# A side program of sliding-window attention in 18 steps in place of 26, at a lower rate of steps

## The chip, the cores and the metric

The kernel runs on one core of a Trainium2 chip. The metric is the device time of one execution in microseconds. The kernel before takes 1376.13 us, the median of three runs (1376.1 to 1376.48).

## The reference

One pass over 512 positions of width 1024 through a block with three mixers, a feed-forward layer with a short convolution, then an mLSTM layer and a layer of dilated attention. The change touches the part of the first block that computes two of the mixers. The sliding-window attention has 8 query heads of width 64 over 2 key heads, in query blocks of 128 positions that each read their own key block and the one before:

```python
s = jnp.einsum('bnqhgd,bnkhd->bnhgqk', qb, kw)
s = jnp.where(valid[None, :, None, None], s, -jnp.inf)
m = jnp.maximum(jnp.max(s, axis=-1, keepdims=True), sink)
p = jnp.exp(s - m)
denom = jnp.sum(p, axis=-1, keepdims=True) + jnp.exp(sink - m)
o = jnp.einsum('bnhgqk,bnkhd->bnqhgd', p / denom, vw)
```

The gated linear attention (GLA) beside it works in chunks of 64 positions with a decay per channel; its output is normalised per head and multiplied by `silu(r)`. The output of each mixer goes through a projection and is multiplied by a sigmoid gate, and the three are added.

## The kernel before

The stream of the large products is what the whole kernel is built around. All weights stand as 128x128 blocks in one long row (`wall`), eight to a unit of 512 KB. SP loads a unit into one of three buffers `raw`; ACT rounds it to fp32r (`WH`, a CAST at L189), DVE computes the rest (`WL = raw - WH`, L152); PE then multiplies each block three times, `HH,WH`, `HL,WH` and `HH,WL` (the activations are split in the same way), each 128x512 (`passes`, L205 is the line of the helper that issues all of them). One block is three matmuls. A tile of the output is 8 blocks of an input of width 1024 or 4 of one of width 512, and takes one of three PSUM banks in turn.

Everything that is no large product is written as a Python generator, a side program, once for each engine: PE, DVE, ACT and POOL each have their own `swa_side()` and `gla_side()`, whose steps (the code between two `yield`) have to be cut alike. The place of a step in the stream is the same on all engines. `tile` calls `pump(0.25)` after every second block; `pump` adds `rate * share` to a counter and takes one step from the first side program of the list for each whole that it holds. With a rate of 1.7 that is 0.425 of a step per turn of two blocks. `tokens` (the four tiles of GLA's values, 32 blocks of weights) makes sixteen such turns, and the narrow tile `glow` four. `later()` runs other short pieces once or twice a tile.

So a step on DVE or ACT stands in its instruction order between the work for the tiles around it: rounding the weights (`CAST WH`, `WL`), and taking finished tiles out of PSUM. Each engine works its list in order, and waits for the others by semaphores.

The sliding attention has eight pieces (`i` from 0 to 7: four query blocks `n`, two pairs of heads `jp`). The parts of one piece, with the engine:

- `scores(i)`: PE, 8 matmuls `ps<-SKT,SQT` (4 for each `ps` bank) into banks 3 and 4 of PSUM. DVE then adds the mask into `SC` (L152), takes the maximum (L170) and three small ones; ACT takes four exponentials of `SC` with their sums (`exps(i)`, L202); DVE divides `SC` by the sum (three instructions, the last `SC<-SC,sm`).
- the transposes of the piece: PE, 8 `ps<-ident,SC` (L209) into banks 5 and 6, and ACT copies them into `PTT` (L189).
- `values(i)`: PE, 16 matmuls `ps<-PTT,SVT` into bank 7; ACT rounds the result into `PH`, DVE computes `PL`.

In each round PE issues `scores(i + 1)`, then in the next step `values(i - 1)`, and in a third one the transposes of `i`. With one step ahead of the rounds and one behind them that makes 26 steps.

GLA follows in the same list. It has two pairs of heads `pr`; for each there are seven levels of masked products in `level(pr, lv)` (PE `ps<-GQK` and `ps<-gqks`, two levels in every second step; POOL and DVE prepare a decay `gE`, ACT takes its exponential, DVE multiplies `gqks<-GQK,gE` and picks the result into `gA`), then the states (`gS`), the outputs (`go`, in banks 3 and 4), and the normalisation: squares, transposes and a sum (`sm`, L170), ACT `Sqrt`, DVE reciprocal (L183), two transposes `ps<-ident,sm` on PE that spread the factor as a row, an ACT copy `RT<-ps`, and DVE `gon<-ps,cv,RT` (L164), which frees the bank of `go`. The first step of levels of the pair `pr = 1` writes into those banks.

The stream beside them: the tile `glow` (blocks 80 to 88), four tiles `gq`, `gk` (to 120), the value tiles (to 152), `branch(0)` (to 248: tiles of 8 and 4 blocks in turn), four tiles `r` (to 280), `branch(1)` (to 376), where POOL also adds into `X` after every second tile.

Of the kernel before, what the change touches and what calls it, by code (L numbers as in the profile page):

```python
# [603 lines left out]
def build(nc, a_in):  # L604
    with ExitStack() as ctx:
# [275 lines left out]
        def pe_program(p):  # L881
# [18 lines left out]
            def swa_side():  # L900
                def scores(i):
                    n, jp = divmod(i, 2)
                    W = 128 if n == 0 else 256
                    k0 = 0 if n == 0 else (n - 1) * P
                    two = [p.fill(SB[g], ("ss", i, g)) for g in range(2)]
                    for jj in range(2):
                        j = 2 * jp + jj
                        p.wait_ge(S.dve, "sq", j)
                        for g in range(2):
                            p.matmul(two[g][:, jj * 256:jj * 256 + W], SQT[64 * g:64 * g + 64, j, n * P:(n + 1) * P],  # L910
                                     SKT[64 * g:64 * g + 64, k0:k0 + W], True, True)
                            if jj:
                                p.then_inc(("ss", i, g))

                def values(i):
                    n, jp = divmod(i, 2)
                    W = 128 if n == 0 else 256
                    k0 = 0 if n == 0 else (n - 1) * P
                    s = p.fill(SB[4], ("so", i))
                    p.wait_ge(S.act, "ptt", i, 1)  # L920
                    for jj in range(2):
                        for q in range(W // P):
                            kb = k0 // P + q
                            p.wait_ge(S.act, "sv")
                            for g in range(2):
                                p.matmul(s[64 * g:64 * g + 64, jj * P:(jj + 1) * P], SVT[:, kb, 64 * g:64 * g + 64],
                                         PTT[:, 2 * g + jj, q * P:(q + 1) * P], q == 0, q == W // P - 1).then_inc(("so", i))

                scores(0)
                yield  # L930
                for i in range(8):
                    n, jp = divmod(i, 2)
                    W = 128 if n == 0 else 256
                    sc = SCS[i % 2][:, :, 0:W]
                    if i < 7:
                        scores(i + 1)
                    yield
                    if i > 0:
                        values(i - 1)
                    yield  # L940
                    for g in range(2):
                        s = p.fill(SB[2 + g], ("st", i, g))
                        p.wait_ge(S.dve, "sn", i)
                        for jj in range(2):
                            for q in range(W // P):
                                p.transpose(s[:, jj * 256 + q * P:jj * 256 + (q + 1) * P], sc[:, 2 * g + jj, q * P:(q + 1) * P], ident)
                        p.then_inc(("st", i, g))
                    yield
                values(7)
                yield  # L950
                p.mark("swa")

            def decays():
                for pr in range(2):
# [217 lines left out]
            p.soon.append(sv_turn())  # L1172
            for j in range(4):
                p.tile(("sq", j), H_mix)
            p.rate = 1.7
            swa = swa_side()
            p.side.append(swa)
            p.narrow(("glow",), H_mix)
# [281 lines left out]
        def dve_program(v):  # L1460
# [17 lines left out]
            def swa_side():  # L1478
                def scores(i):
                    n, jp = divmod(i, 2)  # L1480
                    W = 128 if n == 0 else 256
                    sc = SCS[i % 2][:, :, 0:W]
                    mx, nm, sume, den, es = swa_cols(i)
                    for g in range(2):
                        x = ps("ss", i, g).rearrange("p (j k) -> p j k", j=2)[:, :, 0:W]
                        m = swm[:, 256 - W:256].rearrange("p (o k) -> p o k", o=1).to_broadcast([P, 2, W])
                        v.wait_ge(S.pe, "ss", i, g)
                        v.wait_ge(S.consts, "consts")
                        if i > 1:
                            v.wait_ge(S.pe, "st", i - 2, 1)  # L1490
                        v.tensor_tensor(sc[:, 2 * g:2 * g + 2, :], x, m, ADD).then_inc(("sc", i, g), free("ss", i, g))
                    sinks = cv[:, COL["sinks"] + 4 * jp:COL["sinks"] + 4 * jp + 4]
                    v.wait_ge(S.dve, "sc", i, 1)
                    v.tensor_reduce(mx, sc, MAX).then_inc(("smx", i))
                    v.wait_ge(S.dve, "smx", i)
                    v.tensor_tensor(mx, mx, sinks, MAX).then_inc(("smx2", i))
                    v.wait_ge(S.dve, "smx2", i)
                    v.tensor_scalar(nm, mx, -1.0, MUL).then_inc(("snm", i))
                    v.wait_ge(S.dve, "snm", i)
                    v.tensor_tensor(es, sinks, nm, ADD).then_inc(("ses", i))  # L1500

                def values(i):
                    n, jp = divmod(i, 2)
                    hi = PH[:, 4 + 2 * jp:6 + 2 * jp, n * P:(n + 1) * P]
                    lo = PL[:, 4 + 2 * jp:6 + 2 * jp, n * P:(n + 1) * P]
                    v.wait_ge(S.act, "so hi", i)
                    v.tensor_tensor(lo, ps("so", i)[:, 0:256].rearrange("p (j k) -> p j k", j=2), hi.bitcast(F32),
                                    SUB).then_inc(("sy", i), free("so", i))

                scores(0)  # L1510
                yield
                for i in range(8):
                    W = 128 if i < 2 else 256
                    sc = SCS[i % 2][:, :, 0:W]
                    mx, nm, sume, den, es = swa_cols(i)
                    v.wait_ge(S.act, "sexp", i)
                    v.tensor_tensor(den, sume, es, ADD).then_inc(("sden", i))
                    v.wait_ge(S.dve, "sden", i)
                    v.reciprocal(den, den).then_inc(("srcp", i))
                    v.wait_ge(S.dve, "srcp", i)  # L1520
                    v.tensor_tensor(sc, sc, den.rearrange("p (h o) -> p h o", o=1).to_broadcast([P, 4, W]), MUL).then_inc(("sn", i))
                    if i < 7:
                        scores(i + 1)
                    yield
                    if i > 0:
                        values(i - 1)
                    yield
                    yield
                values(7)
                yield  # L1530
                v.mark("swa")

            def gla_side():
                def output(h):
# [378 lines left out]
            for j in range(4):  # L1913
                v.tile(8)
                v.wait_ge(S.pe, "sq", j)
                v.scalar_tensor_tensor(SQT[:, j, :], ps("sq", j), 0.125, RS, MUL, MUL).then_inc(("sq", j), free("sq", j))
            v.rate = 1.7
            swa = swa_side()
            v.side.append(swa)
            v.tile(8)  # L1920
# [335 lines left out]
        def act_program(a):  # L2256
# [8 lines left out]
            def swa_side():  # L2265
# [10 lines left out]
                def values(i):  # L2276
                    n, jp = divmod(i, 2)
                    a.wait_ge(S.pe, "so", i)
                    a.copy(PH[:, 4 + 2 * jp:6 + 2 * jp, n * P:(n + 1) * P],
                           ps("so", i)[:, 0:256].rearrange("p (j k) -> p j k", j=2)).then_inc(("so hi", i))  # L2280
# [2 lines left out]
                yield  # L2283
                for i in range(8):
                    W = 128 if i < 2 else 256
                    yield
                    if i > 0:
                        values(i - 1)
                    if i < 7:
                        exps(i + 1)  # L2290
                    yield
                    for g in range(2):
                        a.wait_ge(S.pe, "st", i, g)
                        if i > 0:
                            a.wait_ge(S.pe, "so", i - 1)
                        x = ps("st", i, g).rearrange("p (j k) -> p j k", j=2)[:, :, 0:W]
                        a.copy(PTT[:, 2 * g:2 * g + 2, 0:W], x).then_inc(("ptt", i, g), free("st", i, g))
                    yield
                values(7)
                yield  # L2300
                a.mark("swa")

            def decays():
                yield
# [248 lines left out]
            a.soon.append(sv_turn())  # L2553
            for _ in range(4):
                a.tile(8)
            a.rate = 1.7
            swa = swa_side()
            a.side.append(swa)
            a.tile(8)
# [247 lines left out]
        def pool_program(g):  # L2807
# [21 lines left out]
            def swa_side():  # L2829
                yield  # L2830
                for i in range(8):
                    yield
                    yield
                    yield
                yield
                g.mark("swa")

            def gla_side():
                def open_level(pr, lv):
# [54 lines left out]
            g.side.append(pool)  # L2894
            for _ in range(5):
                g.tile(8)
            g.rate = 1.7
            swa = swa_side()
            g.side.append(swa)
            g.tile(8)  # L2900
# [403 lines left out]
```

## Time and profile before

| | us |
|---|---|
| median of three runs | 1376.13 |
| the profiled execution | 1375.52 |
| its span, first to last instruction | 1373.7 |
| PE busy (matmuls) | 1363.2 (99%) |
| PEld busy (weight loads) | 1112.9 (81%) |
| DVE busy | 842.8 (61%) |
| ACT busy | 603.5 (44%) |
| POOL busy | 180.4 (13%) |

The profiled execution is one run of the same program, taken by the hardware profiler; its time of 1375.52 us is 0.61 us below the median. Busy time is the time in which an engine has an instruction in flight. Matmuls overlap: one 128x512 matmul is shown with some 0.39 us and the next starts 0.23 us later, so a busy PE can still lose time between two starts, and starts are the better measure of it. The chain that ended last has 87% of the span on PE, 8% on DVE, 2% on ACT.

### The profile page before, as it was taken

The numbers are of one execution on the slowest core, as the hardware profiler recorded it, in microseconds if no ns is written. First come the engines' busy times: TensorE is split into PE (matmuls) and PEld (weight loads), VectorE is DVE, ScalarE is ACT, GpSimd is POOL, SyncE is SP. The second block draws the span as 40 slices with busy tenths as digits, with TensorE's granted clock in tenths as the row PEclk, the third lists the DMA queues.
The fourth block names the chain that finished last, engine by engine and source line by source line (L and its number), as shares of the span: only waits on it lengthen the run. The fifth ranks groups of instructions, "written<-read, shape, count | busy, mean of one in ns | idle before, by whom it ended". The sixth has DMA issues, their size and how long they took to land.

```text
span 1373.7 us, 17229 instructions
## 1 busy us (share of the span) xinstructions
PE 1363.2 (99%) x6752; PEld 1112.9 (81%) x6752; DVE 842.8 (61%) x1233; ACT 603.5 (44%) x922; POOL 180.4 (13%) x149
## 2 busy tenths in 40 slices
PE   9999999999999999999999999999999999999998
PEld 8777788788888788888888888888888888787887
DVE  6565575854343697624776456746455676877775
ACT  5355433333245454423444345434554544344551
POOL 0300010212311300000000112000001120243330
PEclk9999999999999999999999999999999999999999
DMA  6322222223352433332333324522225233212132
GB/s 213 123 78 77 78 78 62 78 76 94 93 184 77 138 108 108 108 103 82 92 106 94 110 80 150 154 77 77 62 65 175 82 122 100 89 62 63 47 138 77
DMA packets 37817, 136.55 MB, mean 99 GB/s; under 512 B 4452, under 2 KB 5476, under 8 KB 37096
## 3 DMA queue, kind: packets, MB, share of 16 engines
q1 hardware_dynamic: 37440, 134.39, 30.8%
q8 instruction: 53, 0.87, 0.3%
q10 hardware_dynamic: 296, 1.06, 0.2%
q14 instruction: 28, 0.23, 0.1%
HBM read 129.14 MB, written 6.30 MB: 99 GB/s over the span
## 4 chain that ended last, share of the span: by engine, by line
PE 87%; DVE 8%; ACT 2%; issue 2%; DMA 1%; POOL 0%; DVEq 0%; SPq 0%; ACTq 0%; POOLq 0%
PE ps L205 84%; PE ps L209 2%; DVE WL L152 2%; DVE TT L164 2%; DVE HL L164 1%; DMA kept<-PW 1%; DVE X L152 1%; DVE KT L164 0%; ACT WH L189 0%; ACT L202 0%; DVE sm L170 0%; DMA raw<-in_wall 0%; ACT HH L202 0%; DVE gqks L152 0%; ACT row L202 0%
## 5 line engine op out<-in xcount | busy, mean ns | idle before, releaser
L205 PE MATMUL ps<-HH,WH 128*128 128x512 f32 (+1 forms) x1096 | 437.4, 401 | 0.7 <-DVE HL L164 0.6
L205 PE MATMUL ps<-HL,WH 128*128 128x512 f32 (+1 forms) x1096 | 423.4, 388 | 0.0
L205 PE MATMUL ps<-HH,WL 128*128 128x512 f32 (+1 forms) x1080 | 417.6, 388 | 0.0
L152 DVE TENSOR_TENSOR WL<-raw,WH 128x1024 fp32r<-128x1024 f32 (+1 forms) x221 | 282.0, 1281 | 78.2 <-ACT WH L189 77.1
L189 ACT CAST WH<-raw 128x1024 fp32r<-128x1024 f32 (+1 forms) x222 | 231.1, 1042 | 133.9 <-PE ps L205 114.7
L205 PEld LDWEIGHTS ps<-HH,WH 128*128 128x128 f32 x1096 | 205.9, 188 | 48.2 <-issue 6.4
L205 PEld LDWEIGHTS ps<-HL,WH 128*128 128x128 f32 x1096 | 206.2, 188 | 41.4 <-issue 1.9
L205 PEld LDWEIGHTS ps<-HH,WL 128*128 128x128 f32 x1080 | 202.7, 188 | 42.9
L205 PE MATMUL ps<-PH,WH 128*128 128x512 f32 x424 | 167.0, 394 | 0.0
L205 PE MATMUL ps<-PH,WL 128*128 128x512 f32 x424 | 165.2, 390 | 0.0
L205 PE MATMUL ps<-PL,WH 128*128 128x512 f32 x424 | 165.1, 389 | 0.0
L152 POOL TENSOR_TENSOR SQS<-SQS,SQ 128x512 f32<-128x512 f32 x47 | 72.0, 1532 | 677.3 <-ACT SQ L202 676.7
L152 DVE TENSOR_TENSOR TH<-ps,RS 128x512 f32<-128x512 f32 (+1 forms) x93 | 63.6, 684 | 132.7 <-PE ps L205 124.0
L205 PEld LDWEIGHTS ps<-PH,WL 128*128 128x128 f32 x424 | 79.6, 188 | 16.8
L205 PEld LDWEIGHTS ps<-PH,WH 128*128 128x128 f32 x424 | 79.6, 188 | 16.6 <-issue 0.7
L205 PE MATMUL ps<-WH,HH 128*128 128x512 f32 x224 | 91.9, 410 | 0.6 <-DVE WL L152 0.3
L205 PEld LDWEIGHTS ps<-PL,WH 128*128 128x128 f32 x424 | 79.7, 188 | 15.8
L205 PE MATMUL ps<-WL,HH 128*128 128x512 f32 x224 | 87.4, 390 | 0.0
L205 PE MATMUL ps<-WH,HL 128*128 128x512 f32 x224 | 87.3, 390 | 0.0
L202 ACT ACTIVATE TH<-TH 128x512 f32<-128x512 f32 (+1 forms) x41 | 25.5, 621 | 102.1 <-DVE TH L152 102.1
L164 DVE SCALAR_TENSOR_TENSOR CT<-TH,cv,CT 128x511 f32<-128x511 f32 x88 | 65.8, 748 | 6.5 <-ACT CT L202 5.0
L202 ACT ACTIVATE CT<-TH,cv 128x512 f32<-128x512 f32 x44 | 36.0, 818 | 56.7 <-DVE TH L152 54.6
(224 smaller groups left out, 1440.6 us busy)
## 6 DMA issues: line engine op xcount, KB each, us to landing
raw<-in_wall SPq DMA_DIRECT2D x221, 512.0 KB, 3.6
kept<-PW SPq DMA_DIRECT2D x2, 2048.0 KB, 8.9
PWR<-kept SPq DMA_DIRECT2D x2, 2048.0 KB, 7.9
X<-in_xT SPq DMA_DIRECT2D x8, 256.0 KB, 4.1
X<-in_xT SPq DMA_DIRECT2D x4, 512.0 KB, 5.7
out_T<-X SPq DMA_DIRECT2D x7, 256.0 KB, 2.0
pe<-in_pT SPq DMA_DIRECT2D x2, 512.0 KB, 4.9
MB<-mrow ACTq DMA_DIRECT2D x1, 1024.0 KB, 4.8
```

Source lines behind the costliest of these rows:

```text
L152: return self.put(None if self.e is None else self.e.tensor_tensor(out, x, y, op))
L164: return self.put(self.e.scalar_tensor_tensor(out=out, in0=x, scalar=s, in1=y, op0=op0, op1=op1))
L189: return self.put(None if self.e is None else self.e.copy(out, x))
L202: return self.put(self.e.activation(out, x, f, **kw))
L205: return self.put(None if self.e is None else self.e.matmul(out, l, r, start=start, stop=stop, skip_group_check=True))
L209: return self.put(None if self.e is None else self.e.transpose(out, x, ident[0:k, 0:k]))
```

## The change

On every engine the step with `values(i - 1)` and the one with `scores(i + 1)` become one, values first. A round has two steps in place of three, the whole 18 in place of 26. The rate of steps is 1.15 from the start of the sliding attention, and 1.7 again when its last step has returned, which is seen only when the next step is asked for.

```diff
--- before.py
+++ after.py
@@ -932,11 +932,10 @@
                     n, jp = divmod(i, 2)
                     W = 128 if n == 0 else 256
                     sc = SCS[i % 2][:, :, 0:W]
+                    if i > 0:
+                        values(i - 1)
                     if i < 7:
                         scores(i + 1)
-                    yield
-                    if i > 0:
-                        values(i - 1)
                     yield
                     for g in range(2):
                         s = p.fill(SB[2 + g], ("st", i, g))
@@ -949,6 +948,7 @@
                 values(7)
                 yield
                 p.mark("swa")
+                p.rate = 1.7
 
             def decays():
                 for pr in range(2):
@@ -1172,7 +1172,7 @@
             p.soon.append(sv_turn())
             for j in range(4):
                 p.tile(("sq", j), H_mix)
-            p.rate = 1.7
+            p.rate = 1.15
             swa = swa_side()
             p.side.append(swa)
             p.narrow(("glow",), H_mix)
@@ -1525,10 +1525,10 @@
                     if i > 0:
                         values(i - 1)
                     yield
-                    yield
                 values(7)
                 yield
                 v.mark("swa")
+                v.rate = 1.7
 
             def gla_side():
                 def output(h):
@@ -1914,7 +1914,7 @@
                 v.tile(8)
                 v.wait_ge(S.pe, "sq", j)
                 v.scalar_tensor_tensor(SQT[:, j, :], ps("sq", j), 0.125, RS, MUL, MUL).then_inc(("sq", j), free("sq", j))
-            v.rate = 1.7
+            v.rate = 1.15
             swa = swa_side()
             v.side.append(swa)
             v.tile(8)
@@ -2283,12 +2283,11 @@
                 yield
                 for i in range(8):
                     W = 128 if i < 2 else 256
-                    yield
                     if i > 0:
                         values(i - 1)
+                    yield
                     if i < 7:
                         exps(i + 1)
-                    yield
                     for g in range(2):
                         a.wait_ge(S.pe, "st", i, g)
                         if i > 0:
@@ -2299,6 +2298,7 @@
                 values(7)
                 yield
                 a.mark("swa")
+                a.rate = 1.7
 
             def decays():
                 yield
@@ -2553,7 +2553,7 @@
             a.soon.append(sv_turn())
             for _ in range(4):
                 a.tile(8)
-            a.rate = 1.7
+            a.rate = 1.15
             swa = swa_side()
             a.side.append(swa)
             a.tile(8)
@@ -2831,9 +2831,9 @@
                 for i in range(8):
                     yield
                     yield
-                    yield
                 yield
                 g.mark("swa")
+                g.rate = 1.7
 
             def gla_side():
                 def open_level(pr, lv):
@@ -2894,7 +2894,7 @@
             g.side.append(pool)
             for _ in range(5):
                 g.tile(8)
-            g.rate = 1.7
+            g.rate = 1.15
             swa = swa_side()
             g.side.append(swa)
             g.tile(8)
```

No instruction is added or removed; their order changes. Three places show it.

PE, in `branch(0)`, at the values of piece 5 (`ps<-PTT,SVT`). Before:

```order
L205 MATMUL ps<-HL,WH 128x512
L205 MATMUL ps<-HH,WL 128x512
L205 MATMUL ps<-PTT,SVT 64x128 x8
L205 MATMUL ps<-HH,WH 128x512
L205 MATMUL ps<-HL,WH 128x512
```

Now:

```order
L205 MATMUL ps<-HL,WH 128x512
L205 MATMUL ps<-HH,WL 128x512
L205 MATMUL ps<-PTT,SVT 64x128 x8
L205 MATMUL ps<-SKT,SQT 128x256 x4
L205 MATMUL ps<-HH,WH 128x512
L205 MATMUL ps<-HL,WH 128x512
```

The scores of piece 7 (`ps<-SKT,SQT`) stood alone twelve matmuls ahead of the values; now they follow them without a matmul of the stream between. The same holds for six rounds, `i` from 1 to 6.

ACT, at the end of the first GLA pair (`RT<-ps` copies the rows, `PH<-RG` rounds the output, `TH` is the tanh of a tile, the table load goes with `Sqrt` and with the tanh after it). Before:

```order
L202 ACT_TABLE_LOAD
L202 ACTIVATE sm<-sm,cv 128x8
L189 COPY RT<-ps 128x512
L189 CAST PH<-RG 128x512
L202 ACT_TABLE_LOAD
L202 ACTIVATE TH<-RG 128x512
L189 CAST WH<-raw 128x1024
L189 COPY RT<-ps 128x512
L189 CAST PH<-RG 128x512
```

Now:

```order
L202 ACT_TABLE_LOAD
L202 ACTIVATE sm<-sm,cv 128x8
L202 ACT_TABLE_LOAD
L202 ACTIVATE TH<-RG 128x512
L189 CAST WH<-raw 128x1024
L189 COPY RT<-ps 128x512
L189 CAST PH<-RG 128x512
L189 COPY RT<-ps 128x512
L189 CAST PH<-RG 128x512
```

The tanh of the last `r` tile and a rounding of weights stood between the two row copies; now both stand ahead of the first, and the two copies have only `PH<-RG` between them.

POOL, at the second GLA pair (`gb_93` is its decay). Before:

```order
L152 TENSOR_TENSOR gE_83<-gb_93 128x8x32
L152 TENSOR_TENSOR gE_84<-gb_93 128x16x16
L152 TENSOR_TENSOR gE_83<-gb_93 128x32x8
L152 TENSOR_TENSOR gE_84<-gb_93 128x64x4
L152 TENSOR_TENSOR X<-X,TT 128x512
L152 TENSOR_TENSOR gE_83<-gb_93 128x128x2
L152 TENSOR_TENSOR gE_84<-gb_93 128x256
L152 TENSOR_TENSOR X<-X,TT 128x512 x15
```

Now:

```order
L152 TENSOR_TENSOR gE_83<-gb_93 128x8x32
L152 TENSOR_TENSOR gE_84<-gb_93 128x16x16
L152 TENSOR_TENSOR gE_83<-gb_93 128x32x8
L152 TENSOR_TENSOR X<-X,TT 128x512
L152 TENSOR_TENSOR gE_84<-gb_93 128x64x4
L152 TENSOR_TENSOR gE_83<-gb_93 128x128x2
L152 TENSOR_TENSOR gE_84<-gb_93 128x256
L152 TENSOR_TENSOR X<-X,TT 128x512 x15
```

The first addition into `X` stood behind the fourth preparation `gE`, and now stands ahead of it, behind the third.

## Rows read from the trace of the kernel before

**Rows 1.** The page's first part: the span, and busy time of each engine.

```profile
span 1373.7 us, 17229 instructions
PE 1363.2 (99%) x6752; PEld 1112.9 (81%) x6752; DVE 842.8 (61%) x1233; ACT 603.5 (44%) x922; POOL 180.4 (13%) x149
```

**Rows 2.** Two stretches, columns: us; PE, PEld, DVE, ACT, POOL busy (x instructions); clock; DMA.

```profile
66.00:178.00 112.00, 112.00 (x613) 86.69 (x612) 66.51 (x114) 56.46 (x131) 0.00 (x0) 1.00 0.26 81
238.00:300.00 62.00, 59.84 (x499) 48.24 (x499) 43.24 (x71) 23.96 (x34) 12.67 (x8) 1.00 0.22 69
```

**Rows 3.** Who waited for whom, PE: us in total, times, longest.

```profile
PE ps L205 <- DVE gon L164: 1.5, 1, 1.5
```

**Rows 4.** PE in order of time, 149 to 152 us: start, us, engine, instruction.

```profile
149.84 0.39 PE L205 MATMUL ps<-PL,WH 128*128 128x512 f32 x1
150.07 0.39 PE L205 MATMUL ps<-PH,WL 128*128 128x512 f32 x1
150.39 1.14 PE L205 MATMUL ps<-SKT,SQT 64*128 64x256 f32 x8
151.45 0.50 PE L205 MATMUL ps<-HH,WH 128*128 128x512 f32 x1
151.79 0.40 PE L205 MATMUL ps<-HL,WH 128*128 128x512 f32 x1
```

**Rows 5.** PE in order of time: four transposes alone, and four beside two others.

```profile
1166.62 0.60 PE L209 MATMUL ps<-ident,SQ 128*128 128x128 f32 x4
1166.97 0.47 PE L205 MATMUL ps<-HH,WH 128*128 128x512 f32 x1
...
1209.27 0.60 PE L209 MATMUL ps<-ident,SQ 128*128 128x128 f32 x4
1209.71 0.38 PE L209 MATMUL ps<-ident,PB 128*128 128x128 f32 x2
```

**Rows 6.** All engines in order of time, 243 to 249 us, in brackets idle time before.

```profile
243.88 0.60 PE L209 MATMUL ps<-ident,sm 128*128 128x128 f32 x4
...
245.94 1.04 ACT L189 CAST WH<-raw 128x1024 fp32r<-128x1024 f32 x1
...
246.84 0.39 PE L205 MATMUL ps<-HH,WL 128*128 128x512 f32 x1
246.89 0.57 ACT L189 COPY RT<-ps 128x512 f32<-128x512 f32 x1
247.82 0.74 DVE L164 SCALAR_TENSOR_TENSOR gon<-ps,cv,RT 128x512 f32<-128x512 f32 x1
...
248.71 0.69 PE L205 MATMUL ps<-GQK 64*64 64x64 f32 x32 [1.48 <-DVE gon L164]
```

**Rows 7.** PE in order of time, the row transpose of 240 us.

```profile
240.65 0.54 PE L209 MATMUL ps<-ident,sm 128*128 128x128 f32 x3 [0.16 <-DVE sm L183]
```

**Rows 8.** All engines in order of time, 256 to 264 us.

```profile
256.44 2.54 POOL L152 TENSOR_TENSOR X<-X,TT 128x512 f32<-128x512 f32 x1 [4.51 <-DVE TT L164]
...
258.94 2.35 POOL L152 TENSOR_TENSOR gE<-gb 128x256 f32<-128x256 f32 x2
...
261.30 1.23 DVE L152 TENSOR_TENSOR gqks<-GQK,gE 128x1024 f32<-128x1024 f32 x1 [0.48 <-ACT gE L202]
...
263.35 0.69 PE L205 MATMUL ps<-gqks 64*64 64x64 f32 x32 [0.43 <-DVE gA L180]
```

**Rows 9.** All engines in order of time, 151 to 167 us.

```profile
151.55 1.29 DVE L152 TENSOR_TENSOR SC<-ps,swm 128x512 f32<-128x512 f32 x2 [1.54 <-PE ps L205]
...
155.83 0.51 ACT L202 ACTIVATE SC<-SC,sm 128x256 f32<-128x256 f32 x1
...
158.27 1.04 PE L209 MATMUL ps<-ident,SC 128*128 128x128 f32 x8
...
158.91 1.07 ACT L189 COPY PTT<-ps 128x512 f32<-128x512 f32 x2 [0.90 <-PE ps L209]
...
166.07 1.09 PE L205 MATMUL ps<-PTT,SVT 128*64 128x128 f32 x16
```

## The prediction

> **What bounds the kernel.** The page's first part comes first: PE has matmuls in flight for 1363.2 of a span of 1373.7 us [rows 1]. The reader should see that no engine can be relieved with profit unless PE loses time to it. What is left to gain is time between two matmuls of the stream, so the next views are PE in order of time and the table of its waits. The starts of two 128x512 matmuls lie 0.23 us apart (149.84 to 150.07 [rows 4]); a block of three takes 0.68 us. A burst of small matmuls costs more than itself: the last matmul ahead of it takes 0.32 us to the next start (150.07 to 150.39) and the first one behind it 0.34 us (151.45 to 151.79), so each burst has 0.09 + 0.11 = 0.20 us at its two edges [rows 4]. The windows say where PE really stands still: in the sliding attention (66 to 178 us) never, in 238 to 300 us for 62.00 - 59.84 = 2.2 us [rows 2]. The longest wait there is for DVE's `gon` [rows 3], then come shorter ones [rows 7, 8]. The granted clock is 1.00 in both stretches, the level of 2.4 GHz [rows 2], and as PE stays as busy as it was, no term below is one of the clock.
>
> **Part 1: bursts that are joined.** Six times the values burst and the scores burst follow each other, so six pairs of edges go. Between the two bursts something may stay. Four transposes alone take 0.35 us to the next start (1166.62 to 1166.97), four ahead of another burst 0.44 us (1209.27 to 1209.71), so an inner edge of 0.09 us at most is seen [rows 5]. A joined pair saves 0.11 to 0.20 us; I take 0.16, since the only inner edge read is one between transposes and here there are none: 6 x 0.16 = **-1.0 us**, bounds -0.7 and -1.2. The matmuls themselves stay as they are.
>
> The Trainium skill speaks against this term: its page "TensorE: Matmul & The Clock Gate", section "Step-by-step: what each phase is for", says that a weight load is pulled ahead of the matmuls in flight, so that the next weights load under the present matmul. By that rule a burst has no edges and the term is 0; the 0.20 us of the rows say otherwise for this mix of small and large matmuls.
>
> **Part 2: the sliding attention's own waits.** The steps are now 1/(1.15 x 0.25) = 3.5 turns of two blocks apart in place of 2.35, which is 6 to 8 blocks. Values of a piece come one step behind its transposes, not two. That is a new demand on ACT, which sits between them. One piece shows the times: scores at 150.39 us [rows 4], DVE starts on the mask at 151.55, ACT's exponentials begin at 155.83; for another piece the transposes are at 158.27, the copy to `PTT` from 158.91 for 1.07 us, and the values only at 166.07 [rows 9]. Now the values stand 6 blocks behind the transposes there: some 0.8 us of transposes, 0.2 of edges, 6 x 0.68 = 4.1, thus 5.1 us. The copy is done 158.91 + 1.07 - 158.27 = 1.7 us behind the start of the transposes [rows 9]. It can be late only if the exponentials of the next piece, which stand ahead of it on ACT, are. Those follow the scores by 155.83 - 150.39 = 5.4 us here, of which much was the wait for the values of that step, and take 2.2 us (four such rows of 0.51 us, their sums between). Scores to values of the piece before is two steps: some 14 x 0.68 = 9.5 us and 3.2 us of bursts and edges, 12.7. The chain needs at most 1.1 (the values burst ahead of the scores) + 5.4 + 2.2 + 1.1 = 9.8. So 2.9 us are in hand, and I cost this part at **0**. The cover is the stream itself: were the steps closer, PE would stand. The queues behind it: on ACT the weight rounding and the tanh, on DVE `WL`; both are made three units (16 us of stream) ahead. SP issues its loads in the same order as before. POOL has nothing in these steps.
>
> **Part 3: GLA begins later.** Count turns from block 80. Before, step 27 is the first whole beyond 26 steps at 0.425 each: turn 64. Sixteen turns belong to the value tiles, and four each to `glow` and the tiles, which gives block 208. Now 18 steps at 0.2875 end at turn 63, and the rate goes back to 1.7 only when a 19th step is asked for: turn 67, block 214. From there both have the same rates, so that each GLA step comes 6 blocks (4.1 us) later in the stream, its last at 352 and not 346. The output is first read at block 384, so 32 blocks or 22 us are left: no cost. But the steps now meet other work of their engines.
>
> The row copies. Before, the second row transpose was at 243.88 us, and ACT was busy with a table load, the tanh of an `r` tile and a rounding (245.94, 1.04 us) until it copied the row at 246.89; DVE's `gon` came at 247.82, and PE, ready after its matmul of 246.84, began the first level at 248.71: 1.87 us from start to start where an edge has 0.32, a wait of 1.55 us [rows 6]. Now both row steps lie in and at the end of the tile after `r`, and tanh and rounding stand ahead of the first copy. From the second row transpose on it is 0.4 us + 0.6 copy + 0.7 `gon`, with latencies of some 0.1 us between, about 2 us, against 4 blocks = 2.7 us and the burst: the wait goes, **-1.55**. The evacuation of the next gate tile is late instead, by `gon` and two more DVE instructions, some 2.5 us; PE takes that bank again 12 blocks or 8 us later.
>
> The reciprocal. PE waited 0.16 us for it [rows 7]. It now has 8 blocks behind the squares, and ACT's table load stands ahead of nothing else: **-0.16**.
>
> Levels 4 and 5 of the second pair. PE waited 0.43 us; in front of it POOL's addition took 2.54 us, then two `gE` 2.35, and DVE's `gqks` had to wait until 261.30 [rows 8]. Now the addition delays the fourth `gE` and not the fifth. What comes of the fourth is multiplied a whole DVE step (4 blocks, 2.7 us) earlier than what comes of the fifth, while PE reads both in one step, levels 4 and 5. The addition's 2.54 us fit into that step, so I take the wait as gone: **-0.4**, with 0 as the other end, because the two `gE` of 2.35 us stay close ahead of level 5.
>
> What is late next: the states `gS` of the first pair, which DVE made in one go and which are now cut in two by an `r` tile, with `go` close behind. I allow **+0.2** for waits of this sort.
>
> The side programs after GLA keep their number of steps; the fraction left in the counter moves some by a turn or more (mLSTM, dilated attention), each with the same bursts. The same edges and no wait beyond 0.6 us stand there now; **0**, bounds +-0.5.
>
> **Sum.** -1.0 - 1.55 - 0.16 - 0.4 + 0.2 = -2.9 us. Against the profiled execution's 1375.52 us that is 1372.6; that execution lies 0.61 us below the median of the runs shown, so on the footing of the median it is 1373.2 us. A measurement of this kernel tells 0.2% (2.75 us) from no change, and the forecast lies just beyond that line (1373.4).
>
> **Rivals.** (a) *GLA's waits stay in sum.* PE stands still 2.2 us in 238 to 300 us [rows 2]; other places may take that up, since DVE is busy 43.24 of the 62 us there. For it: the POOL addition of 2.54 us is moved earlier in the chain. Against it: the order of ACT takes the cause of the largest wait away. Only part 1 is left: 1376.13 - 1.0 = 1375.1.
> (b) *More is gained.* All waits of the stretch go, and the joined bursts lose their full edges: -1.2 - 2.2 = -3.4, with 0.5 more from the later side programs -3.9: 1372.2 to 1372.7.
> (c) *The edges are not there to be saved*, as if weight loads were pulled ahead inside the new order: the mechanism is that the second burst keeps an edge of 0.20 us. Then the sum is -2.9 + 1.0 = -1.9: 1374.2. The inner edge of 0.09 us speaks against it [rows 5].
> The rule of the Trainium skill's page "TensorE: Matmul & The Clock Gate" named above would give this time.
> (d) *Slower: the copy to `PTT` comes late.* The place is PE's values in the six joined steps, the price what exceeds the 2.9 us in hand. On ACT and DVE a tile can stand in the chain: `WL` (1.2), a rounding (1.04), a tanh and two evacuations of some 0.7 each, 4.3 us. If all of it falls in, each of six rounds waits 1.4 us: +8.4 - 2.9 = +5.5, or 1381.6; if only half the rounds see it, +4.2 - 2.9 = +1.3, 1377.4. It decides from the point where the extra work exceeds 2.9 us. Against it: PE never waits there now, and the 5.4 us hold a wait already.
>
> **Chances.** Forecast (a gain of 2.4 to 3.4 us, 1372.7 to 1373.7) 0.46, (b) 0.18, (a) 0.23, (c) 0.08, (d) 0.05. The range leaves out (d), and of (a) and (b) the ends beyond their bounds: 1372.0 to 1375.3. Faster by over 0.2%: all of (b) and some 0.7 of the forecast's case, 0.18 + 0.32 = 0.50. Slower: 0.03, the worse half of (d). Within 0.2%: the rest, 0.47.
>
> **What would show it.** Right: in 66 to about 178 us PE again without idle time, `ps<-PTT,SVT` followed by `ps<-SKT,SQT` with no stream matmul between, six times, with an interval of 1.0 to 1.1 us for the first; the wait for `gon` gone from PE's table; PE busy over 61.5 of 62 us in the stretch from 238 us. Wrong: PE's waits name `PTT` or `SC` (d), or `gqks`, `gS` and `gon` in new places with over 1 us (a). A wait that appears in the mLSTM or the dilated attention would break the 0 of part 3.

## The result, and the profile after

The change makes the kernel slower: 1380.63 us (median of six runs, 1378.97 to 1381.87) against 1376.07 us of before on the same chip (six runs, 1375.55 to 1376.48). The ratio is 1.0034, 95% interval 1.0024 to 1.0045. Forecast were 1373.2 us, range 1372.0 to 1375.3, with a chance of 0.03 for slower. The profiled execution took 1380.95 us, its span is 1379.1 us.

The page's first part, after:

```profile
span 1379.1 us, 17222 instructions
PE 1364.6 (99%) x6752; PEld 1115.8 (81%) x6752; DVE 843.3 (61%) x1233; ACT 602.9 (44%) x922; POOL 178.2 (13%) x149
```

Against [rows 1] the span is 5.4 us longer and PE's busy time only 1.4 us, so 4 us are time in which PE stands still. The two stretches of [rows 2], after (us; PE, PEld, DVE, ACT, POOL busy; clock; DMA):

```profile
66.00:178.00 112.00, 111.68 (x616) 87.80 (x616) 66.74 (x114) 55.88 (x131) 0.00 (x0) 1.00 0.25 81
238.00:300.00 62.00, 62.00 (x514) 50.70 (x512) 45.12 (x74) 24.72 (x35) 13.46 (x9) 1.00 0.24 77
```

The second stretch is full, where it had 2.2 us idle. The first has 0.3 us of idle time that it had not. The time is lost elsewhere, and the table of PE's waits (us in total, times, longest) names the places at once:

```profile
PE ps L209 <- POOL PB L152: 3.3, 2, 3.1
PE ps L209 <- DVE HU L164: 2.7, 1, 2.7
...
PE ps L205 <- DVE GQK L164: 0.3, 1, 0.3
```

The wait for `gon` of [rows 3] is gone. The first two lines are new. `HU` belongs to the mLSTM at 1007 us, `PB` to the dilated attention at 1208 us, both in parts of the program that the diff does not touch. The line on `GQK` is new too (80 us).

To see where time is won and lost I compare when PE reaches the same matmul in two kernels. The first 40 us, in which nothing differs, already vary by up to 1.2 us between executions (the first matmul of `plw` starts at 39.84 to 41.02 us), so I count from that matmul. Offset to before, in us (minus: earlier), for all kernels below:

| kernel | 179 us | 323 us | 749 us | 1032 us | 1300 us |
|---|---|---|---|---|---|
| the change | -0.89 | -4.09 | -4.12 | +0.11 | +5.15 |
| c1_phase_back | -0.91 | -4.09 | -4.09 | -4.09 | -4.14 |
| c2_phase_only | -0.03 | -0.07 | -0.07 | +4.22 | +10.82 |
| c3_mlstm_only | +0.01 | -0.02 | -0.04 | +4.48 | +4.45 |
| c4_att_only | -0.04 | -0.08 | -0.09 | -0.03 | +0.44 |
| c5_join_only | -0.79 | -0.80 | -0.82 | -0.75 | -0.78 |
| c6_later_only | -0.06 | -3.26 | -3.27 | -3.14 | -3.15 |
| c7_wait_filled | -0.80 | -4.00 | -4.01 | +2.40 | +7.89 |
| c8_pool_count | -0.81 | -4.01 | -4.02 | +0.60 | +1.08 |
| c9_wait_filled_12 | -0.88 | -4.09 | -4.09 | -1.12 | +4.38 |

Each column is the matmul of the stream that starts at that time in the kernel before. So the change wins 4.1 us by 323 us, more than the forecast's 2.9. It then loses 4.2 us at the mLSTM and 5.0 us at the attention.

PE in order of time at the mLSTM, after:

```profile
1006.96 0.49 PE L209 MATMUL ps<-ident,HU 128*128 128x128 f32 x3
1010.10 0.48 PE L209 MATMUL ps<-ident,HU 128*128 128x128 f32 x1 [2.65 <-DVE HU L164]
...
1011.23 0.63 PE L205 MATMUL ps<-WL,HH 128*128 128x512 f32 x1
1011.65 0.63 PE L205 MATMUL ps<-WH,HH 128*128 128x512 f32 x1
```

And before:

```profile
1013.34 0.73 PE L209 MATMUL ps<-ident,HU 128*128 128x128 f32 x4
1013.82 0.48 PE L205 MATMUL ps<-WH,HH 128*128 128x512 f32 x1
```

Before, the four transposes of `HU` follow each other. Now the fourth waits 2.65 us. DVE in order of time says why, after:

```profile
1008.44 0.69 DVE L164 SCALAR_TENSOR_TENSOR TH<-TH,ps 128x512 f32<-128x512 f32 x1 [1.40 <-ACT TH L202]
1009.16 0.88 DVE L164 SCALAR_TENSOR_TENSOR HU<-HU,sm,TH 128x256 f32<-128x256 f32 x2
```

and before:

```profile
1012.08 0.69 DVE L164 SCALAR_TENSOR_TENSOR TH<-TH,ps 128x512 f32<-128x512 f32 x1 [1.40 <-ACT TH L202]
1012.80 0.88 DVE L164 SCALAR_TENSOR_TENSOR HU<-HU,sm,TH 128x256 f32<-128x256 f32 x2
```

The chain that makes `HU` (ACT's tanh, then DVE) comes 3.64 us earlier, as everything there does. PE's step comes 1013.34 - 1006.96 = 6.38 us earlier. The step now has 3986 matmuls of the stream ahead of it and not 3998, which is 12 matmuls, four blocks or two turns of the counter. Before, the second of the two `HU` instructions was done at 1012.80 + 0.88 = 1013.68 us, in the middle of the four transposes. PE had its last operand just in time, and now arrives 2.7 us too soon.

A second loss stands behind the wait. Windows of 3 us, after (columns as above):

```profile
1007.00:1010.00 3.00, 0.45 (x4) 0.21 (x2) 1.57 (x5) 2.33 (x3) 0.00 (x0) 0.94 0.21 86
1010.00:1013.00 3.00, 2.90 (x8) 2.32 (x9) 1.93 (x3) 0.69 (x1) 0.00 (x0) 0.50 0.29 48
1013.00:1016.00 3.00, 3.00 (x16) 2.45 (x15) 1.57 (x3) 0.69 (x1) 0.00 (x0) 0.99 0.32 127
```

After the wait the granted clock is 0.50, the level of 1.2 GHz, and the 128x512 matmuls start 0.42 us apart (1011.23 to 1011.65) and not 0.23. In narrower windows the low clock reaches from 1009.7 to 1013.1 us: 3.4 us, of which the first 0.4 still lie in the wait and 3.0 behind it. The attention shows the same picture (PE in order of time, after):

```profile
1208.13 0.40 PE L205 MATMUL ps<-HH,WL 128*128 128x512 f32 x1
1211.67 0.69 PE L209 MATMUL ps<-ident,PB 128*128 128x128 f32 x2 [3.14 <-POOL PB L152]
...
1213.01 0.63 PE L205 MATMUL ps<-HH,WL 128*128 128x512 f32 x1
1213.43 0.63 PE L205 MATMUL ps<-HH,WH 128*128 128x512 f32 x1
```

POOL in order of time there, after and then before:

```profile
1208.87 1.27 POOL L152 TENSOR_TENSOR QT<-QT,TT 128x512 f32<-128x512 f32 x1 [6.84 <-DVE QT L164]
1210.09 0.72 POOL L152 TENSOR_TENSOR PB<-SS 128x256 f32<-128x256 f32 x1
1210.89 0.72 POOL L152 TENSOR_TENSOR PB<-SS,PB 128x256 f32<-128x256 f32 x1
```

```profile
1206.12 1.30 POOL L152 TENSOR_TENSOR QT<-QT,TT 128x512 f32<-128x512 f32 x1 [4.54 <-DVE QT L164]
1207.38 0.73 POOL L152 TENSOR_TENSOR PB<-SS 128x256 f32<-128x256 f32 x1
1208.19 0.74 POOL L152 TENSOR_TENSOR PB<-SS,PB 128x256 f32<-128x256 f32 x1
```

POOL's order is the same: an addition for `QT`, then the two for `PB`. But that addition waits for DVE, whose own order has moved. `PB` is done at 1211.6 and not at 1208.9 us, while PE's step stands earlier.

### The profile page after: what moved, and what is told of

Same layout as the page of the kernel before. It is cut to its first block and busy times, and to the rows that moved or that the text cites. A ratio compares the mean times of both kernels' runs of the same rounds, so it can differ in the third digit from the quotient of the medians.

```text
span 1379.1 us, 17222 instructions
## 1 busy us (share of the span) xinstructions
PE 1364.6 (99%) x6752; PEld 1115.8 (81%) x6752; DVE 843.3 (61%) x1233; ACT 602.9 (44%) x922; POOL 178.2 (13%) x149
## 3 DMA queue, kind: packets, MB, share of 16 engines
q10 hardware_dynamic: 296, 1.06, 0.2%
```

## Theories

*The counter.* The fraction left in the step counter decides at which turn every later side step falls. By the counting rule it is 0.7 before and 0.4875 after at block 376, 0.20 and 0.9875 in the mLSTM (block 1232), 0.45 and 0.2375 where the attention begins (block 1576). The lost time comes from that alone. It would come without any change to the sliding attention, and go if the fraction is put back.

*Rivals.* The losses come from work that now runs 4 us earlier against the loads of the weights; or the joined steps and the later start leave some other order behind that needs both.

## Experiments

**The fraction put back, and the fraction alone.** c1 is the change with one line on each engine at the end of `branch(1)`, behind GLA:

```diff
+            p.share = 0.7
```

> The changed kernel, with the counter of steps set to 0.7 on every engine behind GLA (block 376), the value that it has there in the kernel before; from there on both have the same order of instructions. Theory A, the loss comes from the fraction carried in the counter into the mLSTM and the dilated attention: the trace after stands 3.8 us ahead of the one before at block 376, so 1376.1 - 3.8 = 1372.3 us, no wait for HU or PB over 0.5 us. Rival B, the loss comes from what the change does near the sliding attention (buffers, DMA, clock) and only shows later: the two waits stay, 1380 us.

Measured: 1371.14 us against 1375.70 of before on its chip, ratio 0.9965 (0.9953 to 0.9978). Faster than both kernels, and by 0.8 us more than was expected. Neither wait appears, and the offset stays between -4.09 and -4.14 to the end. PE at the place, c1:

```profile
1009.51 0.73 PE L209 MATMUL ps<-ident,HU 128*128 128x128 f32 x4
1010.00 0.48 PE L205 MATMUL ps<-WH,HH 128*128 128x512 f32 x1
```

c2 is the opposite: the kernel before, with the change's fraction.

```diff
+            p.share = 0.4875
```

> The kernel before with nothing of the change, but the counter set to 0.4875 behind GLA, the value that the changed kernel has there. Theory A: both waits appear, 4.2 us at the turns of the mLSTM and 5.0 us in the attention: 1376.1 + 9.2 = 1385.3 us. Rival B: 1376.1 us, no change.

Measured: 1385.44 us, ratio 1.0068 (1.0053 to 1.0083), the granted clock over the span 0.996. PE's waits, c2:

```profile
PE ps L209 <- POOL PB L152: 3.3, 2, 3.1
PE ps L209 <- DVE HU L164: 2.7, 1, 2.7
```

One number on each engine, which orders nothing differently before block 378, makes both waits to the tenth of a microsecond and costs 9.7 us in the median, 10.8 in the trace. The rivals need the sliding attention to be changed or the stream to be early; here it is neither. The counter is the cause.

The trace of c2 loses 4.3 us at the mLSTM as the change does, but 6.6 at the attention against 5.0, behind a wait of the same length. What differs is the clock. The 7 us behind the wait's end, the change (mLSTM, attention), then c2 and c9 (a later run) at the attention, and c8 (also later) at the mLSTM:

```profile
1010.10:1017.10 7.00, 7.00 (x27) 5.73 (x28) 3.40 (x5) 2.06 (x3) 0.00 (x0) 0.79 0.26 75
1211.67:1218.67 7.00, 7.00 (x25) 5.15 (x26) 3.07 (x8) 1.73 (x3) 1.73 (x2) 0.80 0.00 0
1215.93:1222.93 7.00, 7.00 (x19) 4.94 (x19) 1.74 (x4) 1.42 (x2) 1.73 (x2) 0.57 0.00 0
1210.79:1217.79 7.00, 7.00 (x23) 4.93 (x24) 2.78 (x8) 1.42 (x2) 1.74 (x2) 0.76 0.00 0
1010.34:1017.34 7.00, 7.00 (x26) 5.64 (x27) 3.40 (x5) 1.84 (x3) 0.00 (x0) 0.76 0.20 75
```

In c2 the low clock lasts 6.8 us at the attention (1215.1 to 1221.9), in the others 3.4. In c9 and c8 it starts only 1.4 and 0.4 us behind the wait's end, so that all of it falls on work, where in the change 0.4 and 0.6 us of it lie in the wait. The losses follow: 5.5 us for c9 at the attention, 4.6 for c8 at the mLSTM. What sets the start and the length stays open.

**Either place alone.** c3 sets the fraction at the mLSTM and puts it back to 0.45 where the attention begins; c4 sets only the attention's, on all four engines.

```diff
+            p.share = 0.4875
...
             p.rate = 4.5
+            p.share = 0.45
```

> The kernel before with the counter at 0.4875 behind GLA and set back to its old 0.45 ahead of the attention. Theory A with two independent places: the wait for HU alone, +4.2 us, 1380.3 us. If the attention's wait came from the mLSTM's delay and not from the counter there, +9.2 us, 1385.3. Rival B: 1376.1.

Measured: 1378.66 us, ratio 1.0023 (1.0014 to 1.0032). One wait, for `HU`, 2.7 us; the offset goes from -0.04 to +4.48 and stays there. A miss in size: the median rises by 3.0 us only, the profiled execution by 4.0, where 4.2 were expected. The record gives the granted clock over the span for each execution, and it shows a reason: the low clock does not follow the wait in every one. A span with 1.000 has room for at most 1.4 us of it. Two of the ten executions of c3 have 1.000 and took 1378.0 and 1378.3 us; the two with 0.998 took 1379.5 and 1379.8. (That all ten waited is taken over from the trace; only one execution has one.)

```diff
             p.rate = 4.5
+            p.share = 0.2375
```

> The kernel before with the counter set to 0.2375 (in place of 0.45) ahead of the attention alone. Theory A with two independent places: the wait for PB alone, +5.0 us, 1381.1 us. If it needed the mLSTM's delay: no change, 1376.1. Rival B: 1376.1.

Measured: 1376.42 us, ratio 1.0005 (0.9996 to 1.0014). A miss: the wait for `PB` does not come, and 0.5 us are lost where 5 were expected. The reason is in the code. POOL skips the mLSTM's tiles and counts on its own, so at the attention its counter had never held the value of the others. c4 set it as well, and with it POOL's order changed: the two additions for `PB` now stand ahead of the fifth one for `QT`. POOL in order of time, c4, the second of them and the one for `QT`:

```profile
1202.70 1.59 POOL L152 TENSOR_TENSOR PB<-SS,PB 128x256 f32<-128x256 f32 x1
1208.19 1.29 POOL L152 TENSOR_TENSOR QT<-QT,TT 128x512 f32<-128x512 f32 x1 [3.90 <-DVE QT L164]
```

The new theory: the wait is made by POOL's order against that of the others, not by the step's place alone. c8 tests it.

**POOL's counter alone.** The change, and one line on POOL where the attention begins:

```diff
             g.rate = 4.5
+            g.share = 0.2375
```

> The change, with the counter of GpSimd alone set to 0.2375 where the dilated attention sets its rate; the three other engines are left as in the change. That moves GpSimd's copy of PB<-SS ahead of the fifth group of additions for QT. If the wait of 3.1 us for PB comes from GpSimd doing these additions first while the other engines' steps stand a turn earlier, the wait and the slow clock behind it go: 5.0 us less than the change (about 1375.6), the offset at the end then near +0.4 like that at the mLSTM. If instead the wait is for the scores or for VectorE's masks, which the other engines' steps set, the wait stays or moves to another instruction and the time is 1380 to 1381.

Measured: 1375.89 us against 1375.93, ratio 0.9999 (0.9990 to 1.0008). PE at the place, c8:

```profile
1208.65 0.39 PE L205 MATMUL ps<-HH,WL 128*128 128x512 f32 x1
1208.88 0.38 PE L209 MATMUL ps<-ident,PB 128*128 128x128 f32 x2
1209.02 0.48 PE L205 MATMUL ps<-HH,WH 128*128 128x512 f32 x1
```

The wait is gone, and the clock stays up there. The loss at the attention is 0.5 us, not 5.0. That settles the second place: PE's, DVE's and ACT's steps moved by a turn, POOL's did not, and POOL did an addition first that no one needed yet. The 5.0 us are thus 3.1 of wait, the 0.5 that is left in c8, and some 1.4 behind the wait, of clock.

The mLSTM's wait is still in this kernel, and again the low clock follows it in some executions only: four of the eleven have 1.000 over the span and took 1374.16 to 1375.01 us, the seven with 0.999 took 1375.86 to 1376.93.

**The two halves of the change.** c5 joins the steps, but lets the sliding attention end where it did, so that GLA begins at block 208 again:

```diff
-            p.rate = 1.15
+            p.rate = 1.19
...
                 p.rate = 1.7
+                p.share = 0.2
```

> The joined steps alone: the sliding attention has its 20 steps and ends at the same block as in the kernel before (rate 1.19, fraction of the counter set to 0.2 where it ends), so everything behind it stands as in the kernel before. If the local terms are those of the prediction, this gains Part 1 alone: 1.1 to 1.3 us less than before (about 1374.5 beside 1375.7), the wait for gon near 241 us stays at 1.8 us, and neither the wait for HU nor that for PB appears. If joining buys nothing (the edges are not saved), it is within 0.3 us of before. If the extra slack of fewer step boundaries counts for more, the offset behind 323 us is beyond -1.5.

Measured: 1375.06 us against 1375.93, ratio 0.9995 (0.9986 to 1.0003), so the median alone does not tell it from no change. The offset is -0.8, where 1.1 to 1.3 were expected; `gon`'s wait is there as it was. (The joined steps are 18; the 20 of the expectation is a slip.) PE in order of time, c5:

```profile
78.97 1.02 PE L205 MATMUL ps<-glow,gup 128*128 128x512 f32 x2
80.31 0.50 PE L205 MATMUL ps<-HH,WH 128*128 128x512 f32 x1 [0.32 <-DVE GQK L164]
...
124.79 1.09 PE L205 MATMUL ps<-PTT,SVT 128*64 128x128 f32 x16
125.82 1.13 PE L205 MATMUL ps<-SKT,SQT 64*128 64x256 f32 x8
126.88 0.50 PE L205 MATMUL ps<-WH,HH 128*128 128x512 f32 x1
```

In the joined pair the values take 1.03 us to the next start and the scores 1.06, just what they take alone (1.02 and 1.06 in the kernel before): an inner edge is not there at all. I count as an edge each start to start between stream and burst that is longer than that of two stream matmuls. From 66 to 185 us these fall from 42 with 4.33 us together to 31 with 3.19, a gain of 1.14. But with the scores elsewhere PE now meets one wait of 0.32 us at 80 us. 1.14 - 0.32 = 0.8 is the offset.

c6 keeps the 26 steps and starts GLA at block 214, by a counter made emptier ahead of the last step of the sliding attention; behind GLA it is set back to 0.7:

```diff
+                p.share = -0.925
                 p.mark("swa")
...
+            p.share = 0.7
```

> The later start alone: the sliding attention keeps its 26 steps at rate 1.7, and the gated linear attention begins at block 214 instead of 208, as in the change; the fraction of the counter behind it is set to 0.7, as it is in the kernel before, so the turn of the mLSTM and the dilated attention stand as before. If the later start takes away the waits for gon and the reciprocals (about 1.9 us) and the burst edges around them, the offset behind 323 us is -2.4 to -2.8 and the time about 1373.1 beside 1375.7. If the joined steps are needed for it, the wait for gon stays and the time is 1375.5 or so. With c5 the two parts should sum to the -3.8 that the run with the fraction put back shows; a sum short of it by over 0.5 us means that the parts work on each other.

Measured: 1372.38 us against 1375.93, ratio 0.9976 (0.9967 to 0.9985); offset -3.15, more than the -2.4 to -2.8 expected. The stretch from 238 us, c6:

```profile
238.00:300.00 62.00, 62.00 (x515) 50.73 (x513) 44.92 (x74) 24.48 (x35) 13.46 (x9) 1.00 0.24 77
```

So the later start alone fills it, and -0.8 and -3.15 sum to -3.95 where c1 has -4.1: the parts are independent. The medians agree within their noise (-0.9 and -3.5; c1: -4.6).

**Is the low clock the wait's doing?** c7 is the change with small multiplications of the identity on PE between the third and the fourth transpose of the mLSTM's first turn, into a bank that nobody reads:

```diff
+                    if (half, i, t) == (0, 0, 3):
+                        idle = p.fill(SB[0], ("idle2",))
+                        for _ in range(26):
+                            p.matmul(idle[:, 0:P], ident, ident, True, True)
+                        p.then_inc("idle2", free("idle2"))
```

> The change, with 26 small multiplications more (128 x 128, identity times identity, into a bank that nobody reads) that TensorE does in the mLSTM while it waits for HU; they add nothing to the result. In the change TensorE waits 2.65 us there and then runs at a granted clock of 0.50 for some 2.5 us. If the clock falls because TensorE stands still, the filled wait keeps the granted clock at 1.0 behind it, the multiplications by then start 0.23 us apart instead of 0.43, and the time is about 1.3 us less than the change's (1379.3 beside 1380.6). If the clock would fall there whatever TensorE does, or the filling outlasts the wait by as much as the clock gives back, the time is that of the change (1380.6) or more.

Measured: 1383.02 us, ratio 1.0050 (1.0035 to 1.0066). It is slower than the change by its offset (+7.89 against +5.15); the intervals of the two ratios overlap. Each of the 26 counts as two in the trace and takes 0.22 us, so they filled 5.8 us and outlasted the wait. But the clock was 1.00 in them and behind them. c9 has 12:

> The change, with 12 small multiplications ahead of the transpose that waits for HU, in place of 26. In the run with 26 they took 5.8 us and so outlasted the wait by 3.1 us, but the granted clock stayed at 1.00 behind them. Twelve take 12/26 of that, 2.7 us, which is the length of the wait. If the low clock comes from TensorE standing still, the wait is covered, the clock stays at 1.00 and some 1.3 us come back: the offset at 1036 us, counted from the first 40 us, is -1.2 (the change: +0.11), and the time about 1.3 us less than the change's. If the low clock has another cause that the longer filling only outlasted, 1010 to 1013 us show 0.50 again and the offset stays at +0.1.

Measured, PE in order of time and two windows of c9:

```profile
1007.77 2.84 PE L205 MATMUL ps<-ident 128*128 128x128 f32 x24
1010.60 0.33 PE L209 MATMUL ps<-ident,HU 128*128 128x128 f32 x1
...
1011.47 0.40 PE L205 MATMUL ps<-WH,HH 128*128 128x512 f32 x1
1011.70 0.39 PE L205 MATMUL ps<-WH,HL 128*128 128x512 f32 x1
```

```profile
1007.00:1010.00 3.00, 3.00 (x26) 2.87 (x25) 1.50 (x5) 2.83 (x3) 0.00 (x0) 1.00 0.30 119
1010.00:1013.00 3.00, 3.00 (x17) 2.43 (x16) 2.43 (x4) 1.33 (x2) 0.00 (x0) 1.00 0.06 11
```

The fourth transpose still comes 3.1 us behind the first three, since DVE is no faster, but the clock stays at 1.00 and the stream's matmuls start 0.23 us apart. The offset at 1032 us is -1.12 against +0.11: 1.2 us come back, by work that computes nothing. So the 4.2 us of the mLSTM are 2.65 of wait, some 1.3 of clock, and a rest of 0.2.

Since the low clock does not follow every wait, one trace with 1.00 could be chance. The clocks over the span speak against it: 0.997 needs at least 6.9 us at the low clock, as two stretches and the end of the run give, where the clock falls too; 0.999 leaves at most 4.1, so one stretch of 3.4 us and not two. The change has 0.997 in four of its six executions, and 0.999 in the other two. The ten executions of c7 and c9, with the mLSTM's wait filled and the attention's left, have 0.999 or 1.000.

The median of c9 does not show the gain (1380.14 us, ratio 1.0033, 1.0021 to 1.0045), a miss. 0.5 us of it is lost again at the attention (-1.12 to +4.38 is 5.5, the change has 5.0), where the low clock fell later, wholly on work, as shown above; and two of the six executions of the change had at most one low stretch themselves. The rest is within what two sets of runs differ by.

The Trainium skill's page "TensorE: Matmul & The Clock Gate", section "HAM oscillation — how this bites in real kernels", describes a kernel in which PE waits for a DMA between its groups of products, and finds the low clock again at the start of each group. The change's trace agrees in kind: 0.50 behind each of its two waits, while c9, with one of them filled, has 1.00 there and 1.2 us less. It differs in that the waits here are 2.65 and 3.14 us, where the section's are 3 to 5, and in that the executions of c3 and c8 with 1.000 over the span have no such stretch of low clock at all.

## Why the prediction was wrong

The sum failed at one step, the last of part 3: "The side programs after GLA keep their number of steps; the fraction left in the counter moves some by a turn or more (mLSTM, dilated attention), each with the same bursts. The same edges and no wait beyond 0.6 us stand there now; 0, bounds +-0.5." It costs +9.3 us in the change (4.2 and 5.0). The text named the very places, and took the absence of waits in the trace of before as slack. It was none. A step that never waits can have its operand just in time: the last `HU` was done at 1013.68 and PE's four transposes began at 1013.34. What had to be read there is how long before the step each operand is done, and what a turn is worth in time. The step moved by two turns, 2.7 us, against a chain that does not move with the counter, and in the attention three engines' steps moved against POOL's, which has a counter of its own. Some 1.3 and 1.4 us of the 9.3 are clock, which the prediction had put at nothing because PE would stay as busy as it was. The bounds of +-0.5 rested on edges and not on these distances, and so no rival had the mechanism. The rival on the slow side, a late copy to `PTT`, did not happen: no wait on `PTT` or `SC` shows.

The other terms, against c5 and c6:

- *Part 1*, forecast -1.0 with bounds -0.7 and -1.2: the edges gave -1.14. The full edges are saved, and the choice of 0.16 per pair was too careful; the rival that no edge is saved fell. The term of 0, which the prediction worked out from a rule of the Trainium skill's page "TensorE: Matmul & The Clock Gate", section "Step-by-step: what each phase is for", is not what this mix shows; how the weight loads lie inside an edge was not measured.
- *Part 2*, forecast 0: no wait in the attention's own chain, but +0.32 in the products of `glow` beside it, whose cover (scores between) the text had not looked at.
- *Part 3, GLA*, forecast -1.9, measured -3.15. `gon` went as forecast (-1.55). The reciprocal's wait stood there twice, once for each pair (240 and 301 us), and each with its edge is worth 0.38: -0.76 in place of -0.16. Levels 4 and 5 gave 0.5, the transposes of `gqks` another 0.3, and the allowance of +0.2 for new waits was not needed. Together they are 3.1 of the 3.2 us that c6 has gained by 323 us.

So even without the counter the forecast would have been too slow, and outside its range. c1 gains 4.6 us by the medians (4.1 by the trace) where 2.9 were forecast; from the 1376.1 of before that is 1371.5, and the range ended at 1372.0. The term that was too small is GLA's in part 3, by 1.2 us.

## What to carry to other kernels

Where one counter or one running sum places all later steps, a local change has to hand the same value on, or the whole rest of the program is reordered; setting it at the seam costs nothing and here was worth 9 us. "No wait there" is not slack: before moving a step, read for each operand how long before the step it is done, on every engine that counts by itself. And a wait of PE of nearly 3 us can cost half as much again in clock behind it, in some executions and not in others, so that one trace of such a kernel does not stand for its median.

## What the hardware showed

- A standstill of 2.65 us (mLSTM) or 3.14 us (attention), of a PE that had no wait over 0.6 us in the 500 us before the first, was followed in every trace that has one unfilled by a granted clock of 0.50, for 3.4 us (once, in c2, 6.8 us), with 128x512 matmuls 0.42 us apart. It began between 0.8 us before the end of the wait and 1.4 us behind it. The wait of 1.48 us (`gon`) had a clock of 1.00 behind it [rows 2, 6].
- The low clock does not follow in every execution: two of ten of c3 and four of eleven of c8 have a clock over the span that leaves no room for it.
- In both traces with small multiplications in the wait (5.97 and 2.84 us of them) the clock stayed at 1.00 behind it.
- Two different bursts of small matmuls, values and then scores, have no edge between them (1.03 and 1.06 us, as alone), while such a burst and the stream have 0.09 us ahead and 0.11 behind. In the trace of before, the transposes of a piece have an edge only behind them: 0.23 us ahead, as between two stream matmuls, and 0.31 behind.
